# A 512-token model block: the first three feature tiles behind each boundary taken in halves, and fewer idle products among the turns

## The reference

```python
for i in range(DEPTH):                     # DEPTH = 2
    m = mixer(x)                           # latent and window attention, or forgetting attention
    x = _layer_norm(DN_ALPHA * x + m, ln1_g[i], ln1_b[i])
    x = _layer_norm(DN_ALPHA * x + square(relu(x @ w_up[i])) @ w_down[i], ln2_g[i], ln2_b[i])
    gate = sigmoid(x @ ple_w_gate[i] + ple_b_gate[i])
    x = x + gate * (p[i] @ ple_w_proj[i])
h = rmsnorm(x, norm1_g)
x = x + concat(gla(h), conv(h)) @ w_out
h2 = rmsnorm(x, norm2_g)
x = x + (silu(h2 @ w_gate) * (h2 @ w_up)) @ w_down
return rmsnorm(x, norm_f_g)
```

## Time and profile before

| | us |
|---|---|
| median of 3 runs (lowest, highest) | 1980.57 (1980.38, 1980.96) |
| the profiled execution's own time | 1980.13 |
| its span, first to last instruction | 1978.3 |
| TensorE busy, share of the span | 98% |
| GpSimd busy | 64% |
| VectorE busy | 44% |
| ScalarE busy | 17% |

### The profile page before, as it was taken

One profiled execution on the slowest core, in us unless ns is written; L12 is line 12 of the kernel. 1 busy time (PEld: TensorE's weight loads), 2 busy tenths in 40 slices (PEclk: granted clock), 3 DMA queues, 4 the chain that ended last, 5 costly groups with the idle time before them and its releaser, 6 DMA issues.

```text
span 1978.3 us, 24552 instructions
## 1 busy us (share of the span) xinstructions
PE 1948.5 (98%) x9180; PEld 1616.7 (82%) x9180; DVE 867.8 (44%) x1208; ACT 327.1 (17%) x627; POOL 1261.5 (64%) x818
## 2 busy tenths in 40 slices
PE   9999999999999999999999999999999999999998
PEld 8788788888887878888788888877888778888886
DVE  2587372253349511472832443377457840000234
ACT  1377200000003100461300000033122130000001
POOL 5576576667767547775566677756553556666674
PEclk9999999999999999999999999999999999999999
DMA  6411233333222323112233233322221223332322
GB/s 222 134 33 33 85 107 96 95 96 117 95 96 85 97 76 107 57 50 86 70 122 95 95 117 95 95 86 86 67 85 64 75 93 98 97 95 95 96 96 75
DMA packets 53698, 181.31 MB, mean 92 GB/s; under 512 B 6584, under 2 KB 9322, under 8 KB 53498
## 3 DMA queue, kind: packets, MB, share of 16 engines
q1 hardware_dynamic: 46656, 165.17, 26.6%
q10 hardware_dynamic: 6970, 15.11, 2.3%
HBM read 176.56 MB, written 3.70 MB: 91 GB/s over the span
## 4 chain that ended last, share of the span: by engine, by line
PE 90%; DVE 4%; POOL 3%; ACT 1%; issue 1%; POOLq 0%; DVEq 0%
PE PS L643 88%; POOL WL L532 1%; PE PS L810 1%; PE PS L889 1%; POOL WH L529 1%; POOL PB L560 1%; DVE STL L1866 0%; DVE X L1600 0%; DVE PS L1583 0%; DVE U L1928 0%; ACT HT L2102 0%; DVE STH L1865 0%; ACT PTH L2053 0%; DVE ST L1875 0%; DVE PTL L1513 0%
## 5 line engine op out<-in xcount | busy, mean ns | idle before, releaser
L532 POOL TENSOR_TENSOR WL<-RW,WH 128x1024 fp32r<-128x1024 f32 x301 | 762.7, 2534 | 25.1
L529 POOL TENSOR_SCALAR WH<-RW 128x1024 fp32r<-128x1024 f32 x301 | 351.5, 1168 | 629.3 <-PE PS L643 607.9
L643 PE MATMUL PS<-XTH,WH 128*128 128x512 f32 x1168 | 456.9, 391 | 2.1 <-DVE XTL L1633 1.6
L643 PE MATMUL PS<-XTL,WH 128*128 128x512 f32 x1168 | 454.7, 389 | 0.0
L643 PE MATMUL PS<-XTH,WL 128*128 128x512 f32 x1168 | 454.6, 389 | 0.0
L643 PE MATMUL PS<-WL,HSH 128*128 128x512 f32 x688 | 267.5, 390 | 2.1 <-POOL WL L532 2.1
L643 PE MATMUL PS<-WH,HSL 128*128 128x512 f32 x688 | 267.7, 389 | 0.0
L643 PE MATMUL PS<-WH,HSH 128*128 128x512 f32 x688 | 267.7, 389 | 0.0
L643 PEld LDWEIGHTS PS<-XTH,WH 128*128 128x128 f32 x1168 | 219.2, 188 | 50.6 <-DVE XTL L1633 3.7
L643 PEld LDWEIGHTS PS<-XTH,WL 128*128 128x128 f32 x1168 | 219.3, 188 | 46.0
L643 PEld LDWEIGHTS PS<-XTL,WH 128*128 128x128 f32 x1168 | 219.3, 188 | 44.1
(11 more groups left out here) (337 smaller groups left out, 2309.2 us busy)
## 6 DMA issues: line engine op xcount, KB each, us to landing
RW<-stream SPq DMA_DIRECT2D x302, 512.0 KB, 3.6
BC<-gate_rows SPq DMA_DIRECT2D x16, 256.0 KB, 3.3
G<-gain_rows ACTq DMA_DIRECT2D x5, 512.0 KB, 3.5
X<-x ACTq DMA_DIRECT2D x1, 2048.0 KB, 10.5
G<-bias_vecs ACTq DMA_DIRECT2D x4, 512.0 KB, 5.2
out<-X SPq DMA_DIRECT2D x4, 512.0 KB, 2.7
XS<-xt ACTq DMA_DIRECT2D x3, 512.0 KB, 8.7
bias_rows<-QM ACTq DMA_DIRECT2D x1, 1536.0 KB, 6.8
```

The lines of the kernel that those rows point to most:

```text
L529: pool.tensor_scalar(WH[:, j % WS, :], RW[:, j % RAW, :], 1.0, 1.0, ALU.mult, ALU.mult).then_inc(hi_split, 1)
L532: pool.tensor_tensor(WL[:, j % WS, :], RW[:, j % RAW, :], WH[:, j % WS, :].bitcast(F32), ALU.subtract).then_inc(lo_split, 1)
L643: return pe.matmul(o, a, b, start=start, stop=stop)
```

## The change

Behind a boundary the first three feature tiles (`SPLIT_K = 3`) are taken in two halves of the tokens, 256 each. The order of work changes on all three engines:

- TensorE: token tiles 0, 1 and 2 are turned, then `first_group` runs feature tiles 0, 1 and 2 on the first half of the tokens, with token tile 3 turned among them, and then the second half. The banks are first set to zero by `clear`, a product with a tile of zeros that opens the sum. Behind boundaries 1 and 4 it is `gate_half` that takes its tokens so, with the same products as before in another order.
- VectorE splits feature tiles 0 to 2 in halves (`split_half`), and scales token tile 3 (`scale(3)`) only after the first two halves.
- ScalarE copies token tiles 0 and 1 before it does the deviation of tile 3, and gives gains in halves. Ahead of boundaries 0, 3 and 5 it takes one square root of a spare value.
- Most idle products go: boundaries 0 and 3 have 3 where there were 18, boundaries 1 and 4 have 4 of 7, boundary 2 none of 9, boundary 5 has 17 of 32, and boundary 6 has 7 of 19.
- At boundaries 2 and 5 two of the turns share banks with the two before them (`turned_at`).
- Apart from that, the first sums of the forget gates (`forget_sums`) leave out columns whose result is zero: 512, 384, 256 and 128 columns instead of four times 512.

```diff
+SPLIT_K = 3
+HALVES = (slice(0, S // 2), slice(S // 2, S))
+def ready_parts(b, k, half):
+    base = KD + (KD + SPLIT_K) * b
+    return base + (half * SPLIT_K + k + 1 if k < SPLIT_K else SPLIT_K + k + 1)
...
+        ZERO = sb("ZERO", [P, P], F32R)
+        SPARE = sb("SPARE", [P, 1])
...
-            return (t if BOUND[b][0] else (t + 2) % T) * D
+            return (t if BOUND[b][0] else t % 2 + 2) * D
...
+            def clear(bank):
+                mm(PS[:, bank, :].rearrange("p (t n) -> p t n", t=T), ZERO[:, :],
+                   IDLE[:, :].unsqueeze(1).to_broadcast([P, T, P]), True, False)
...
+            def first_group(c, b, turn_tile):
+                def one(k, half):
+                    u, cc = UNIT * (k % 2), c + k // 2
+                    ts = slice(0, S) if half is None else HALVES[half]
+                    pe.wait_ge(xt_ready, ready_parts(b, k, half or 0))
+                    for m in range(4):
+                        w = slice(u + m * P, u + (m + 1) * P)
+                        x = mm3(PS[:, m, ts], WH[:, cc % WS, w], WL[:, cc % WS, w],
+                                XTH[:, k, ts], XTL[:, k, ts], False, k == KD - 1)
+                    return x
+                chunk(c)
+                one(0, 0)
+                if not BOUND[b][0]:
+                    turn_tile(T - 1)
+                one(1, 0)
+                if BOUND[b][0]:
+                    turn_tile(T - 1)
+                chunk(c + 1)
+                one(2, 0)
+                one(0, 1)
+                one(1, 1).then_inc(chunk_used, 1)
+                one(2, 1)
+                for k in range(SPLIT_K, KD):
+                    if k % 2 == 0:
+                        chunk(c + k // 2)
+                    x = one(k, None)
+                    if k % 2:
+                        x.then_inc(chunk_used, 1)
...
+            def turn_tile(b, t):
...
+                if not add and t == 0:
+                    pe.wait_ge(emb_z, 16 if kind else 8)
+                elif not add and t >= 2:
+                    pe.wait_ge(yt_copied, 5 * b + t - 1)
+                src = YN[:, t, :] if kind == "rms" else X[:, t, :]
+                for k in range(KD):
+                    o = turned_at(b, t) + P * k
+                    x = pe.transpose(PSF[:, o:o + P], src[:, k * P:(k + 1) * P], IDENT[:, :])
+                x.then_inc(x_turned, 1)
+            def boundary(b, c, embed=None):
                 add, kind, n = BOUND[b]
                 if kind and not add:
                     pe.wait_ge(emb_z, 16)
                     occupy(4, 8)
-                for t in range(T):
-                    if kind and add and t >= 2:
-                        if kind == "rms":
-                            pe.wait_ge(var_ready, 4 * n + t + 1)
-                            occupy(2 * t, 8 if t == 2 else 2)
-                        elif not embed or t == 2:
-                            pe.wait_ge(yt_copied, 5 * b + 1)
-                            occupy(0, 7 if t == 2 else 2)
-                    elif kind and not add and t:
-                        pe.wait_ge(var_ready, 4 * n + t + 1)
-                        occupy((2 * t + 4) % 8, 5)
...
-                    if embed and t == 2:
-                        pe.wait_ge(yt_copied, 5 * b + 1)
-                        embed(0)
+                    pe.wait_ge(var_ready, 4 * n + T)
+                    occupy(0, 9)
+                turn_tile(b, 0)
+                turn_tile(b, 1)
                 if embed:
+                    pe.wait_ge(yt_copied, 5 * b + 1)
+                    occupy(0, 4)
+                    turn_tile(b, 2)
+                    embed(0)
                     embed(1)
                     pe.wait_ge(yt_copied, 5 * b + 2)
                     embed(2)
+                    turn_tile(b, T - 1)
                     embed(3)
-                    pe.wait_ge(yt_copied, 5 * b + 5)
-                else:
+                    return
+                if add:
+                    pe.wait_ge(yt_copied, 5 * b + 1)
+                    occupy(0, 3)
+                elif not kind:
+                    pe.wait_ge(y_ready, Y_BASE[b] + T)
+                clear(0)
+                clear(1)
+                if not add:
+                    clear(2)
+                    clear(3)
+                turn_tile(b, 2)
+                if add:
                     pe.wait_ge(yt_copied, 5 * b + 2)
-                    occupy(0 if add else 4, 9)
-            def hidden(c, groups, g0, new):
+                    if kind == "rms":
+                        occupy(2, 4)
+                    clear(2)
+                    clear(3)
+                first_group(c, b, lambda t: turn_tile(b, t))
...
+                if b is not None:
+                    pe.wait_ge(yt_copied, 5 * b + 3)
+                    for half in range(2):
+                        if half:
+                            pe.wait_ge(yt_copied, 5 * b + 5)
+                        for k in range(SPLIT_K):
+                            if k % 2 == 0 and not half:
+                                chunk(c + k // 2)
+                            pe.wait_ge(xt_ready, ready_parts(b, k, half))
+                            for t in (2 * half, 2 * half + 1):
+                                x = one(k, t)
+                            if k == 1 and half:
+                                x.then_inc(chunk_used, 1)
+                for k in range(0 if b is None else SPLIT_K, KD - 2):
...
                 for t in range(T):
-                    mm(PS[0:RANK, 4, :], LF[:, RANK * t:RANK * (t + 1)],
-                       STEPS[:, 3 * P - t * P:3 * P - t * P + S], t == 0, t == T - 1)
+                    mm(PS[0:RANK, 4, t * P:], LF[:, RANK * t:RANK * (t + 1)],
+                       STEPS[:, 3 * P:3 * P + S - t * P], t == 0, t == T - 1)
...
+                def split(k, ts=slice(0, S)):
+                    y = YT[:, k, ts]
+                    if k == 0 and layer:
+                        own(ve.tensor_scalar(y, y, GAINS[:, n, 0:1], BIASES[:, n, 0:1], M, A))
+                    elif k == 0 and kind:
+                        own(ve.tensor_scalar(y, y, GAINS[:, n, 0:1], None, M))
+                    own(ve.tensor_copy(XTH[:, k, ts], y))
+                    ve.tensor_tensor(XTL[:, k, ts], y, XTH[:, k, ts].bitcast(F32), SUB).then_inc(xt_ready, 1)
+                def split_half(k, half):
+                    if k and kind:
+                        ve.wait_ge(yt_ready, (KD + SPLIT_K - 2) * n + (SPLIT_K - 1) * half + k)
+                    else:
+                        ve.wait_ge(yt_copied, 5 * b + 2 + 2 * half)
+                    split(k, HALVES[half])
                 if kind:
-                    for t in range(T):
-                        residual(t)
-                        if t and add:
-                            scale(t - 1)
-                    scale(T - 1)
+                    residual(0)
+                    residual(1)
+                    if add:
+                        scale(0)
+                    residual(2)
+                    if add:
+                        scale(1)
+                    residual(3)
+                    if add:
+                        scale(2)
+                    if b == 7 or not add:
+                        scale(3)
                 if b < 7:
...
+                    split_half(0, 0)
+                    split_half(1, 0)
+                    if kind and add:
+                        scale(3)
+                    split_half(2, 0)
+                    for k in range(SPLIT_K):
+                        split_half(k, 1)
+                    for k in range(SPLIT_K, KD):
+                        if kind:
+                            ve.wait_ge(yt_ready, (KD + SPLIT_K - 2) * n + SPLIT_K - 1 + k)
                         else:
-                            ve.wait_ge(yt_copied, 5 * b + 5)
...
+                            ve.wait_ge(yt_copied, 5 * b + (4 if k < KD // 2 else 5))
+                        split(k)
...
-                first_copy = T if kind and not add else 2
-                for t in range(T):
+                def features_ready(k, ts=slice(0, S)):
...
+                if kind and b in (0, 3, 5):
+                    act.activation(SPARE[:, :], EPS[:, 0:1], F.Sqrt)
+                ahead = T if b == 7 or not add else T - 1
+                if kind:
+                    for t in range(ahead):
+                        deviation(t)
+                if b < 7:
+                    copy_out(0)
+                    copy_out(1)
+                if kind and ahead < T:
+                    deviation(T - 1)
+                if b < 7:
                     if kind:
-                        deviation(t)
-                    if b < 7 and t >= first_copy:
-                        copy_out(t - 2)
-                if b < 7:
-                    for t in range(T - 1) if first_copy == T else (T - 2,):
-                        copy_out(t)
+                        act.wait_ge(yt_copied, 5 * b + 2)
+                        for k in range(1, SPLIT_K):
```

(23 more changed lines are left out.)

100 lines of the change are left out of this document (37 added, 63 removed).

## The result

The changed kernel takes 1994.77 us (median of 4 runs, 1994.21 to 1997.39) beside 1980.47 us of the kernel before (4 runs): a ratio of 1.0075, 95% interval 1.0062 to 1.0088. It is slower by 14.3 us, against a forecast of 2.8 us faster and outside the range.

What follows compares the result with a forecast made beforehand. TensorE, busy 98% of the span, was taken as the bound, with idle products at the boundaries to win back. Terms summed to -2.8 us: 1980.13 to 1977.3, plus 0.44 to the median, 1977.8 us; range 1969.5 to 1983.5.

Steps and rivals of the forecast that it cites:

- the last term before the sum: Extra memsets and square roots lie where their engines wait: nothing, at most 0.1 us at the start otherwise.
- the slower case of 0.10: Chance 0.10 of a time over 1984.5 us, mostly from clock falls at boundaries 0, 1, 3, 4 and 6.
- the second rival: Clock falls at boundaries 0 and 3 in TensorE's idle time, 1.8 us each: 1981.4 us; chance 0.15.
- a fall elsewhere than at boundary 5: Sign of being wrong: the granted clock falls at a place other than boundary 5.
- The shared path of VectorE and GpSimd: At boundaries, VectorE working from SBUF and GpSimd alternate by whole instructions; half tiles are held like full ones.
- The first rival: Halves aren't held, or GpSimd gives way: boundaries 0 and 3 give 3.2 each, in all -11.5 us, 1969.1; chance 0.25.
- Boundaries 0 and 3: Early square root and half tiles, with splits held by GpSimd, gain 0.5 us each, -1.0 in all.
- Boundaries 1 and 4: Ahead of the gate, a later last turn and an earlier need for the second chunk cost +2.2 us each, +4.4.
- Boundary 5: Idle products ahead of the turns keep TensorE busy, none slow between them: -5.4 us, about 1.7 of it the clock.
- Boundary 6: First product comes earlier, but 72 half products, a turn and a wait take longer than 36 full ones: +0.7 us.
- Boundary 2 with the forget sums: Boundary 2, bound by TensorE itself, -0.2 us, and the shortened forget gates' sums, -1.3: -1.5 us together.
- The sums themselves: Forget gates' sums leave out 768 of 2048 columns, three eighths of 3.4 us: -1.3 us on TensorE's path.

Runs made afterwards that it cites:

- e10_aligned256: Changed kernel with the unused tile SPARE widened to 256 bytes a partition, putting HSH and HSL a multiple of 256 bytes from WH and WL: 1979.32 us.
- e7_late_cut: Changed kernel with SPARE at 128 bytes, plus GpSimd's second chunk cut held behind the first two half splits at boundaries 0, 3, 6: 1983.92 us against 1993.20.
- e1_aligned: Changed kernel with SPARE widened from 4 to 64 bytes a partition, instructions and order unchanged: 1993.75 us.
- e8_gate_order: Changed kernel with SPARE at 128 bytes, plus boundaries 1 and 4 back in the order of the kernel before: 1989.73 us against 1993.20.

## Why the prediction was wrong

**The step that failed** is the last term before the sum: "The extra memsets and the square roots lie where their engines wait: nothing". It priced the new tiles by the instructions that fill them, not by the bytes they take. They moved the down stages' stationary tiles to 32 bytes off a multiple of 256 from the weights, at 6.4 ns for each of 2064 products: +13.2 us. No rival had it, and the slower case of 0.10 was built on the clock. With the tiles back in place (e10_aligned256) the change gives 1979.32 us against a forecast of 1977.8: in the range, and no change that can be measured.

A second, smaller part went against the sum: the clock fell twice in the profiled execution, at boundaries 0 and 3, some 3 us in all. That was the second rival (0.15) and not the forecast, and the prediction had named a fall elsewhere than at boundary 5 as a sign of being wrong. Of the 14.3 us, 13.2 for the addresses and 3.0 for the clock leave -1.9, against the -2.8 of the sum.

Point by point, by the table:
- *The shared path of VectorE and GpSimd* was right: the halves are held as whole instructions (1.02 and 2.53 us), the first product stood 7.85 us behind the first turn where some 8 were named. The first rival (not held) falls as a forecast; with the hold taken off the first split, e7_late_cut gave 2.4 us each at boundaries 0 and 3, where the rival had 2.7 more than the sum. (The rival's total of -11.5 is a slip: by its own terms it is -12.6.) By the Trainium skill, page "SBUF — State Buffer", section "Who interferes with whom", it is an exclusive lock that one side has for a whole instruction, and what can take it is told by the kind of operation, with no word of its width. These rows agree: a cast of 256 columns took 1.02 us beside WH and 0.28 without. The half split by itself costs 0.41, 0.28 and 0.42, the 1.1 in all that was taken, and products of 256 columns stand 0.12 us apart, as taken (30 of them from 250.07 to 253.66).
- *Boundaries 0 and 3*: the steps came as told, with too much taken for them: without a fall and without the addresses' share boundary 0 gave +0.1 (e10_aligned256) and boundary 3 -0.4, where -0.5 each was forecast. The fall of the clock came on top. In the profiled execution it fell at both, at 1.5 us for the one measured (1.8 named), and e1_aligned shows that the same idle time doesn't always bring it. The pieces add up: +6.5 is 4.9 for the addresses, 1.5 for the clock and 0.1 left, +6.0 is 4.9, 1.5 and -0.4. TensorE's idle time ahead of the fall was 2.5 us (2.7 named).
- *Boundaries 1 and 4*: +2.2 each, measured +2.15. The gate started 12.68 us behind the first turn (12.7 named). The wait for WL twelve products later was there, with 0.6 us of idle time where 1.1 was named. e8_gate_order takes 3.9 of the 4.3 back.
- *Boundary 5*: -5.4, measured -5.3; the first useful product 4.4 us behind the first turn (4.3 named), no stretch at 0.50:
```profile
1390.63 1.97 PE L924 MATMUL PS<-IDENT,HT 128*128 128x128 f32 x16 [0.16 <-DVE HT L1809]
...
1395.02 0.36 PE L657 MATMUL PS<-XTH,WH 128*128 128x256 f32 x1 [0.63 <-DVE XTL L1697]
```
- *Boundary 6*: +0.7, measured +1.1 with the tiles back in place. *Boundary 2 with the forget sums*: -1.5, measured -1.1. The sums themselves gave the -1.3 forecast: from the first of the eight to the product behind them it was 3.54 us before (723.15 to 726.69) and 2.25 after (731.83 to 734.08). So boundary 2 alone is +0.2 in place of -0.2.

What stays open is why the distance counts. The runs have multiples of 256 as fast, and 32, 64, 96, 128, 160 and 224 off one as slow (the last two only by the 96 products on OH and OL); steps below 32 bytes and other types were not tried.

## What to carry to other kernels

A new tile, even one of four unused bytes, moves all tiles allocated behind it. Compare the mean duration of each shape of product before and after, also in stages that the diff doesn't touch, and try the stationary and moving tiles of a hot loop at a multiple of 256 bytes from each other: here it was worth 13 us in 1990. When the first split of a stage is urgent, let the engine that shares VectorE's path start its long operations behind it: here some 2 us at each of three boundaries.

## What the hardware showed that I had not expected

- A product of 512 columns costs 5.4 to 7.4 ns more when its stationary and moving tile don't lie a multiple of 256 bytes apart (busy time of 688 products: 267.5 us at 0, 271.9 at 32 and 64, 272.6 at 96, 271.3 at 128). The weight load itself is as long as before, 188 ns in both of these, of the kernel before and the changed one:
```profile
L643 PEld LDWEIGHTS PS<-WL,HSH 128*128 128x128 f32 x688 | 128.9, 188 | 29.9 <-POOL WL L532 3.4
```
```profile
L657 PEld LDWEIGHTS PS<-WL,HSH 128*128 128x128 f32 x688 | 129.0, 188 | 34.1 <-POOL WL L546 3.1
```
  The Trainium skill, page "TensorE: Matmul & The Clock Gate", section "Step-by-step: what each phase is for", gives TensorE two independent read ports and says that "Loading the next tile's weights doesn't steal SBUF read bandwidth from the running matmul." These rows don't fit that fully: the product's time depends on how far apart the two tiles lie. That it is the two reads which meet is my reading and not shown. The measurement decides.
- The granted clock fell from 1.00 to 0.50 for some 3 to 4 us in one execution and not in another with the same instructions and the same idle time of 2.46 us (changed kernel and e1_aligned, above).
